# Moving the scan's wait on the evicted W products from its first and fifth step to its second and fifth, where they are first read

## What is computed

```
def step(state, inp):
    qg, kd, u_i, w_i, a_i, gl = inp
    v_new = u_i - jnp.einsum('bhcd,bhde->bhce', w_i, state)
    o = jnp.einsum('bhcd,bhde->bhce', qg, state) + jnp.einsum('bhcs,bhse->bhce', a_i, v_new)
    state = state * gl[..., None] + jnp.einsum('bhcd,bhce->bhde', kd, v_new)
    return state, o
s0 = jnp.zeros((B_, H, Dk, Dv), jnp.float32)
_, o = lax.scan(step, s0, xs)
```

## Time and profile before

| | us |
|---|---|
| median of 3 runs (lowest, highest) | 865.08 (862.08, 866.42) |
| the profiled execution: its time | 863.28 |
| the profiled execution: its span | 861.5 |
| TensorE busy in the span | 764.0 |
| VectorE busy | 494.5 |
| ScalarE busy | 462.0 |
| GpSimd busy | 145.3 |
| mean granted clock of TensorE, as a share of full speed | 0.955 |

### The profile page before, as it was taken

How to read it: one execution, slowest core, us unless ns; L and a number is a source line. 1 busy time by engine, 2 the same in 40 slices (tenths; PEclk the granted TensorE clock), 3 DMA queues, 4 the chain that set the end, 5 groups by cost and what they waited for, 6 DMA issues and landing times.

```text
span 861.5 us, 11407 instructions
## 1 busy us (share of the span) xinstructions
PE 764.0 (89%) x3996; PEld 620.6 (72%) x3996; DVE 494.5 (57%) x1068; ACT 462.0 (54%) x1045; POOL 145.3 (17%) x248
## 2 busy tenths in 40 slices
PE   6999969899987999699996999895698998998975
PEld 5888857778876888578895788773476676774764
DVE  5634869756664475544655378763556556536532
ACT  4523566888768875788677852224443334323300
POOL 0000000053021510242101520001002033212330
PEclk9999989999998999899997999997989999999988
DMA  9312110124001320014000241008401122111201
GB/s 357 100 49 75 49 37 26 37 65 141 25 26 49 96 86 25 21 60 127 25 25 25 88 131 49 25 25 266 148 1 49 37 86 86 49 50 61 74 25 49
DMA packets 56424, 60.87 MB, mean 71 GB/s; under 512 B 16048, under 2 KB 42928, under 8 KB 55984
## 3 DMA queue, kind: packets, MB, share of 16 engines
q1 hardware_dynamic: 56368, 60.15, 21.3%
HBM read 45.46 MB, written 14.68 MB: 70 GB/s over the span
## 4 chain that ended last, share of the span: by engine, by line
PE 62%; DVE 19%; ACT 11%; issue 6%; DMA 1%; SPq 0%; POOL 0%; DVEq 0%; ACTq 0%; POOLq 0%
PE bank L846 15%; PE bank L854 9%; PE bank L856 9%; PE bank L855 9%; PE bank L860 3%; ACT cst L1658 3%; PE bank L1090 2%; PE bank L1118 2%; PE bank L1010 2%; DVE score L1280 2%; PE bank L1025 2%; PE bank L997 2%; PE bank L1023 2%; DVE mix_lo L1525 1%; DVE arena L1489 1%
## 5 line engine op out<-in xcount | busy, mean ns | idle before, releaser
L854 PE MATMUL bank<-x_hi,ring_split 128*128 128x512 f32 x480 | 200.9, 419 | 7.4 <-DVE x_lo L1225 7.3
L855 PE MATMUL bank<-x_lo,ring_split 128*128 128x512 f32 x480 | 191.6, 399 | 0.0
L856 PE MATMUL bank<-x_hi,ring_split 128*128 128x512 f32 x480 | 191.6, 399 | 0.0
L1658 ACT ACTIVATE cst<-score,sel 128x1024 bf16<-128x1024 f32 (+2 forms) x192 | 166.9, 873 | 29.0 <-DVE sel L1302 27.6
L854 PEld LDWEIGHTS bank<-x_hi,ring_split 128*128 128x128 f32 x480 | 93.2, 194 | 23.4 <-DVE ring_split L1233 7.2
L856 PEld LDWEIGHTS bank<-x_hi,ring_split 128*128 128x128 f32 x480 | 92.8, 193 | 20.8
L855 PEld LDWEIGHTS bank<-x_lo,ring_split 128*128 128x128 f32 x480 | 93.2, 194 | 15.6
L1759 ACT ACTIVATE arena<-arena,misc 128x512 f32<-128x512 f32 (+7 forms) x32 | 24.8, 775 | 81.0 <-DVE misc L1495 81.0
L1575 ACT ACTIVATE arena<-bank 128x512 f32<-128x512 f32 (+1 forms) x108 | 49.8, 499 | 34.3 <-PE bank L860 9.7
L846 PE MATMUL bank<-w_out_hi,mix_hi 128*128 128x512 f32 x128 | 56.0, 438 | 6.7 <-DVE mix_lo L1525 4.2
L1545 DVE SCALAR_TENSOR_TENSOR arena<-qkvT,bank 128x512 f32<-128x512 f32 x16 | 11.0, 688 | 80.0 <-PE bank L846 80.0
(11 more groups left out here) (247 smaller groups left out, 1438.9 us busy)
## 6 DMA issues: line engine op xcount, KB each, us to landing
ring<-in_w_groups SPq DMA_DIRECT2D x30, 512.0 KB, 3.5
x_raw<-in_x_t SPq DMA_DIRECT2D x8, 512.0 KB, 9.3
side_z<-stage SPq DMA_DIRECT2D x16, 256.0 KB, 2.1
w_out_sb<-in_wout_t SPq DMA_DIRECT2D x2, 2048.0 KB, 13.0
zgT<-side_z SPq DMA_DIRECT2D x8, 512.0 KB, 3.9
qkvT<-in_x SPq DMA_DIRECT2D x8, 512.0 KB, 4.7
out_y<-arena SPq DMA_DIRECT2D x8, 512.0 KB, 2.8
ring<-in_wmem_t SPq DMA_DIRECT2D x2, 1024.0 KB, 4.7
```

Of the source, the lines that this page charges most:

```text
L854: nc.tensor.matmul(dst, hi, xh, start=(c == 0), stop=False)
L855: nc.tensor.matmul(dst, hi, xl, start=False, stop=False)
L856: last = nc.tensor.matmul(dst, lo, xh, start=False, stop=(c == KT - 1))
L1658: sc.activation(signs[order[e] % 2][:, 0:w], score[:, score_at(b):score_at(b + 1)], ACT.Sign, scale=-1.0, bias=candidate[:, b - 2:b - 1], ...
```

## The change

The wait for the evictions of the W products is taken out of the start of steps 0 and 4. It now stands at steps 1 and 4, behind the product of Y with the values, and ahead of the product that reads W.

```diff
                     key = ("V", h, b)
-                    if i == 0:
-                        pe.wait_ge(*released(("nw", h, a)))
                     if not first(key):
                         pe.wait_ge(*vacated(key))
                     last = nc.tensor.matmul(ps(key)[:, 0:P], blk(row(a, R_Y), i), blk(row(a, R_VB), i), start=True, stop=(b == 0))
                     if b:
 
+                        if b == 1 or i == 0:
+                            pe.wait_ge(*released(("nw", h, a)))
                         pe.wait_ge(*released(("S", h, b - 1)))
                         last = nc.tensor.matmul(ps(key)[:, 0:P], blk(row(a, R_NW), i), dn_s[:, (b % 2) * P:(b % 2 + 1) * P], start=False, stop=True)
```

## The result

The changed kernel takes 866.83 us (median of 20 runs, 864.82 to 869.24), the kernel before 863.69 us (20 runs, 861.16 to 866.42): ratio 1.004 (1.0036 from the two medians), interval [1.003, 1.005]. It is slower by 3.1 us; the forecast was +2.7, with bounds of +0.9 and +4.5. The profiled execution has a span of 867.3 us against 861.5.

The account below looks back on a forecast made before the run. TensorE was taken as the bound, busy 764.0 of 861.5 us, so its waits mattered. A gain of 3.7 us and a clock loss of 6.4 us gave +2.7 on 865.08, 867.8 us; 8-in-10 range 862.0 to 871.0.

Parts of the forecast that it names:

- The wait is not removed, it stands 14 instructions later: Scan start: step 0's O product waits for the same W product 0 eviction; about 1.8 us at L1060, then at L1065.
- The gain is 1.23 us a head: ScalarE's copy into hbuf no longer waits for TensorE's first unit, so dn_s comes earlier; 3.7 us over three heads.
- The loss by the clock: TensorE idles right before L1049 and starts the full stretch at half clock: 14.1 us, losing 6.4 us (bounds 4.6 to 8.2).
- the same 0.45: Loss per us of half-clock stretch, from matmuls 0.42 us apart instead of 0.23: 1 - 0.23/0.42 = 0.45 us.
- The forecast's base: Whole kernel before: median of three runs, 865.08 us, to which the sum of +2.7 us was added.
- The page's rule: Half-clock stretches: loss is throttled time times (1 - 1.2/2.4), 7.05 us for 14.1 us, making the sum +3.3 us.
- A clock that stays up: Rival: clock stays or is again full at L1049, leaving only the 3.7 us gain, 861.4 us; chance 0.12.
- The whole 20.5 us: Rival: L1045's whole wait goes, 3 x 6.84 = 20.5 us come off, 844.6 us; chance 0.03.
- A half clock through the whole full stretch of 7.6 us: Rival: from L1049 half clock lasts 7.6 us a head, losing 10.3 us, net +6.6, 871.7 us; chance 0.18.

Follow-up runs that it names:

- e3: Kernel before, waits unmoved, plus unread matmuls in the first three heads: ten ahead of the scan's first wait, three ahead of V of step 1; ratio 0.9961, 859.30 us.
- e2: Changed kernel plus unread matmuls in the first three heads: five ahead of the S product of step 0, eight ahead of V of step 1; ratio 0.996, 859.72 us.
- e8: Changed kernel, W products one piece of work earlier, plus unread matmuls: five ahead of S of step 0, six ahead of V of step 1; ratio 0.9925, 857.64 us.
- e10: Kernel before, wait unmoved, W products one piece earlier, plus unread matmuls: two ahead of the wait, nine ahead of V of step 1; ratio 0.9915, 857.04 us.
- e5: Changed kernel plus five unread matmuls ahead of V of step 1 alone, none ahead of S of step 0; ratio 0.996, 860.51 us.
- e9: Kernel before, wait unmoved, W products one piece earlier, plus unread matmuls: two ahead of the wait, six ahead of V of step 1; ratio 0.9962, 860.14 us.

## Why the prediction was right

- **The wait is not removed, it stands 14 instructions later.** As predicted: L1065 waits for the same copy, 1.46 us in the first head, after 1.85 us at L1060; 1.8 us each were forecast. The transposes behind it ran at half clock already. The work from L1065 to the wait at L1049 took longer than the forecast 2.3 us (2.9 us in the first head), so that wait was 4.07 us there, and not 4.8.
- **The gain is 1.23 us a head.** From the update to L1049 9.33 us were measured against 9.4 forecast, and 10.60 before, 1.27 us less, and as much in the other two heads. e3 shows what this gain is: the half clock that the old wait had laid on the first unit.
- **The loss by the clock.** Forecast from the stretches of before: 14.1 us at half clock, 6.4 us lost. Measured: 15.3 us, which at the same 0.45 is 6.9 us. Less 3.7 that is +3.2; the medians differ by 3.1. So close an agreement is partly luck: the lengths were 5.4, 4.2 and 5.7 us where 4.0, 4.0 and 6.1 were taken, and they come from one execution, which is 2.2 us above its kernel's median (over the 20 runs of the changed kernel the mean granted clock goes from 0.946 to 0.954). The forecast's base, the median of three runs, also lies 1.4 us above that of 20 runs, so the absolute 867.8 is 1.0 us too high though the difference is 0.4 us too small. That the clock is the cause is shown, not argued: e2 keeps every wait instruction and takes the half clock away, and gets the bare gain, -3.5 us from the ratio of 0.996 (forecast -3.7).
- **The page's rule** of a loss of half the throttled time (the Trainium skill, "TensorE: Matmul & The Clock Gate", section "HAM oscillation — how this bites in real kernels") would give 7.7 us for these 15.3, and +4.0, an estimate. The runs here do not decide between it and the rows' 0.45: the interval of the ratio is 2.6 to 4.3 us and holds +3.2 and +4.0, and in the profiled execution the heads took 3.5 us longer in spite of a gain of 3.8, which makes the loss 7.3 us, between 6.9 and 7.7.
- **The rivals.** A clock that stays up was the case of e2 and not of the change. The whole 20.5 us were never to be had: e8 and e10, which have hardly any wait for the copies left, gain 6 to 7 us, the 2.3 us a head by which VectorE's chain to `dn_s` got shorter. A half clock through the whole full stretch of 7.6 us did not come; the longest was 5.7.
- **What the sum did not have to explain.** The two profiled spans differ by 5.8 us, of which 1.5 us lie ahead of the first changed instruction. There both kernels are the same; in the changed kernel's execution at least one half-clock stretch lasts longer there. From where TensorE is ready for V of step 0 to V of step 2 the heads take 21.94, 21.43 and 22.14 us against 20.68, 20.65 and 20.67: 3.5 us in all. The rest is outside the scans' starts. For the first head these are the ends, before and after:

```profile
275.18 0.39 PE L1045 MATMUL bank<-arena 128*128 128x128 f32 x2
```

```profile
277.94 0.39 PE L1043 MATMUL bank<-arena 128*128 128x128 f32 x2
```

They are measured from 254.50 and 256.00.

The stretches of both executions at an early place where the programs are equal; first before, then after:

```profile
118.50:125.30 6.80, 5.15 (x13) 4.24 (x14) 6.23 (x19) 3.60 (x9) 0.00 (x0) 0.50 0.00 0
```

```profile
125.30:128.60 3.30, 3.30 (x11) 3.11 (x10) 1.89 (x4) 3.16 (x6) 0.00 (x0) 0.52 0.00 0
```

The stretch at half clock that ended at 125.3 in the one goes on to 128.6 in the other.

## What to carry to other kernels

Before a wait is moved down an engine's queue, look for the next thing that the engine must wait for there: a bank that comes round in its ring can hold the same wait under another name, and an engine that feeds the next one sets the time anyway. Then ask where the idle time will lie. Here 6.8 us of idle time ahead of work that VectorE's chain covered for the most part cost 1.2 us a head by the half clock behind it. Idle time of 4 to 5 us right ahead of a full stretch put 4 to 6 us of that stretch at half clock, and cost some 2.4 us a head.

## What was not expected

Matmuls of no use made the kernel faster: 13 a head in three heads give 0.4% over the kernel before, in the changed kernel (e2) and in the kernel before (e3), and five a head ahead of V of step 1 do as much (e5). With the W products evicted earlier, 11 a head give 0.8% (e8, e10). And in e9 a half-clock stretch of 3.4 us followed in each head on a wait of 2.22 us, though 4.0 us of full work at clock 1.00 lay ahead of it; in e8 none followed on a wait of 1.26 us.
